# The depthwise convolution of a two-layer hybrid trunk on GpSimd: moved ahead of three weight subtractions, and its multiplications given a second operation

## The reference, cut to what matters

```python
z = _rms(h, norm1_g[l]) @ w_in[l]
ya = _attention_group(za, q_norm_g[l], k_norm_g[l], attn_sinks[l])
yr = _rwkv_group(zr, rwkv_mu[l], ...)
yc = _conv_group(zc, conv_w[l], conv_b[l], conv_ln_g[l], conv_ln_b[l])
h = h + jnp.concatenate([ya, yr, yc], axis=-1) @ w_out[l]
h = h + _peer(_rms(h, norm2_g[l]), peer_wq[l], peer_keys[l], peer_u[l], peer_v[l])

def _conv_group(z, conv_w, conv_b, ln_g, ln_b):
    u = z[..., :CONV_CH] * jax.nn.sigmoid(z[..., CONV_CH:])
    u = lax.conv_general_dilated(u, conv_w[:, None, :], window_strides=(1,), padding=[(CONV_K - 1, 0)],
                                 feature_group_count=CONV_CH) + conv_b
    return jax.nn.silu(_layernorm(u, ln_g, ln_b))
```

## Time and profile before

| What | Value |
|---|---|
| Median of 3 runs | 2122.08 us (2120.01, 2122.08, 2127.78) |
| Span of the profiled execution | 2125.6 us |
| PE busy, of the span | 1976.9 us, 93% |
| DVE busy | 1458.0 us, 69% |
| POOL busy | 1289.0 us, 61% |
| ACT busy | 963.9 us, 45% |
| Mixers of layer 0, from the end of the input projection to the output projection | about 96 to 233 us |
| Mixers of layer 1 | about 1155 to 1297 us |

### The profile page before, as it was taken

One profiled execution on the slowest core, in us unless ns is written; L12 is line 12 of the kernel. 1 busy time (PEld: TensorE's weight loads), 2 busy tenths in 40 slices (PEclk: granted clock), 3 DMA queues, 4 the chain that ended last, 5 costly groups with the idle time before them and its releaser, 6 DMA issues.

```text
span 2125.6 us, 43559 instructions
## 1 busy us (share of the span) xinstructions
PE 1976.9 (93%) x16496; PEld 1888.4 (89%) x16496; DVE 1458.0 (69%) x2763; ACT 963.9 (45%) x1645; POOL 1289.0 (61%) x667
## 2 busy tenths in 40 slices
PE   6857899999999999999998577999999999999999
PEld 6855899999999999999988466999999999999998
DVE  2773419994777788788757634199727777887886
ACT  5512446554333354555554124465543333555553
POOL 3798377998666633233047983789986666332430
PEclk9977899999999999999999679999999999999999
DMA  4400255565444598888743002555654445998995
GB/s 159 124 2 1 80 169 159 179 196 169 147 145 145 152 353 313 289 308 320 241 144 110 1 1 80 179 168 182 185 187 136 145 147 192 347 326 300 311 344 154
DMA packets 106236, 387.48 MB, mean 182 GB/s; under 512 B 11792, under 2 KB 12048, under 8 KB 105744
## 3 DMA queue, kind: packets, MB, share of 16 engines
q1 hardware_dynamic: 87696, 318.93, 45.8%
q0 software_dynamic: 18432, 67.12, 8.6%
HBM read 384.95 MB, written 1.05 MB: 182 GB/s over the span
## 4 chain that ended last, share of the span: by engine, by line
PE 60%; POOL 24%; issue 13%; DVE 1%; ACT 1%; DMA 1%; SPq 0%; POOLq 0%; ACTq 0%
PE ps L881 60%; POOL w_lo L544 14%; POOL arena L560 6%; POOL arena L569 4%; DMA arena<-lora_c 1%; POOL arena L556 0%; ACT w_hi L627 0%; DVE h L1791 0%; DVE x L1371 0%; SPq L509 0%; DVE sel L1677 0%; ACT L745 0%; ACT L602 0%; DVE x_lo L1364 0%; DVE h L1790 0%
## 5 line engine op out<-in xcount | busy, mean ns | idle before, releaser
L881 PE MATMUL ps<-x_hi,w_hi 128*128 128x240 f32 (+5 forms) x4768 | 1435.2, 325 | 29.4 <-POOL w_lo L544 10.7
L881 PE MATMUL ps<-x_hi,w_lo 128*128 128x240 f32 (+3 forms) x4768 | 1306.3, 274 | 0.0
L544 POOL TENSOR_TENSOR w_lo<-w,w_hi 128x1024 fp32r<-128x1024 f32 x346 | 868.1, 2526 | 414.7 <-ACT w_hi L627 414.4
L881 PEld LDWEIGHTS ps<-x_hi,w_hi 128*128 128x128 f32 x4768 | 905.2, 190 | 83.9 <-issue 15.2
L881 PEld LDWEIGHTS ps<-x_hi,w_lo 128*128 128x128 f32 x4768 | 909.8, 191 | 0.0
L627 ACT CAST w_hi<-w 128x1024 fp32r<-128x1024 f32 x596 | 623.2, 1046 | 348.3 <-PE ps L881 223.4
L881 PE MATMUL ps<-x_lo,w_hi 128*128 128x240 f32 (+3 forms) x2720 | 756.4, 278 | 0.0
L881 PEld LDWEIGHTS ps<-x_lo,w_hi 128*128 128x128 f32 x2720 | 519.8, 191 | 0.6
L1748 DVE TENSOR_TENSOR w_lo<-w,w_hi 128x1024 fp32r<-128x1024 f32 x250 | 305.5, 1222 | 114.8 <-ACT w_hi L627 114.4
L881 PE MATMUL ps<-arena 64*64 64x64 f32 (+9 forms) x2496 | 175.3, 276 | 59.7 <-ACT arena L769 21.1
L881 PEld LDWEIGHTS ps<-arena 64*64 64x64 f32 (+6 forms) x2496 | 151.5, 171 | 81.2 <-ACT arena L769 21.7
(11 more groups left out here) (185 smaller groups left out, 1699.1 us busy)
## 6 DMA issues: line engine op xcount, KB each, us to landing
w<-u_c SPq DMA_DIRECT2D x256, 512.0 KB, 3.6
w<-v_c SPq DMA_DIRECT2D x256, 512.0 KB, 4.4
w<-w_c SPq DMA_DIRECT2D x84, 512.0 KB, 3.6
arena<-keys_c SPq DMA_DIRECT2D x2, 1024.0 KB, 6.8
arena<-mix_c SPq DMA_DIRECT2D x2, 632.0 KB, 7.9
h<-h SPq DMA_DIRECT2D x1, 1088.0 KB, 5.1
out<-x SPq DMA_DIRECT2D x4, 256.0 KB, 2.2
arena<-lora_c SPq DMA_DIRECT2D x2, 256.0 KB, 8.0
```

What stands on the lines that cost most here:

```text
L544: g.tensor_tensor(low_of(l, n, wlo_t), low_of(l, n, wraw_t), high_of(l, n).bitcast(F32), ALU.subtract).then_inc(s_lo, 1)
L881: return nc.tensor.matmul(out_, lhsT, rhs, start=start, stop=stop, skip_group_check=True)
```

## The change

The three low halves 18, 19 and 20, which POOL made ahead of the convolution, are made behind it. And the multiplications of taps 1 to 30 get a second operation, the addition of the constant 0.0; tap 0 keeps its bias.

```diff
             for l in range(DEPTH):
-                lows(l, 0 if l == 0 else AHEAD, NZ + AHEAD)
+                lows(l, 0 if l == 0 else AHEAD, NZ)
 
                 pool.wait_ge(s_ea, l * (NZ + NQ) + ZQ)
...
                         ins = g.tensor_scalar(dst[:, j, :], cu[:, j, k:k + T], vcol(l, "conv_w", j * CONV_K + k),
-                                              vcol(l, "conv_b", j) if k == 0 else None, ALU.mult,
-                                              *((ALU.add,) if k == 0 else ()))
+                                              vcol(l, "conv_b", j) if k == 0 else 0.0, ALU.mult, ALU.add)
...
-                lows(l, NZ + AHEAD, NP)
+                lows(l, NZ, NP)
```

## The result

The changed kernel takes 2133.65 us (median of 9 runs), the kernel before 2125.99 us (9 runs). The ratio is 1.0038, with a 95% interval of 1.0026 to 1.005: slower by 8.1 us (5.5 to 10.6), where 2122 was forecast in a range up to 2129. It lies within the 0.5% that I had called no change, and outside the range. Part of the distance to 2122 was in the start of the sum: the three runs it was built on have a median of 2122.08 us, the nine of now 2125.99. The profiled execution after has a span of 2131.8 us against 2125.6; in the run after, the reported time is 1.85 us longer than the span.

A forecast was written before the change was run, and what follows sets the result against it. DVE's attention steps and ACT's exponentials were taken to bound the convolution's end. Ends -3.0, hold-ups in between +2.8 and PE's clock +0.9 gave +0.7 us on 2122.08: 2122 us, range 2112 to 2129.

The forecast's parts named there:

- The end of the convolution was not on the path: End of the convolution, layer 0: covered by DVE's attention until 208.95 and ACT's exponentials; ending 32 us earlier counted 0.
- 6.72 us of TensorE's wait: PE's wait for the convolution's last addition, layer 0: predicted to become waits for DVE, worth 0.
- The hold-ups in DVE's full stretch: DVE at about 110 to 135 us in layer 0: denser POOL additions cost +1.4 us a layer, +2.8 in all.
- ACT's cast within 2 us of 229.26: Sign at the mixers' end: ACT's cast of the mixed tokens stays there; 5 us or more earlier would refute the forecast.
- the 0.56 I took: Multiplication with a second operation on POOL: 0.56 us, like tap 0's, saving 24 us of POOL a layer.
- the 0.96 of the other bound: Multiplication no faster with the constant: 0.96 us, convolution ends at 200; rival forecast 2121 us, chance 0.12.
- the relief at the ends: DVE rows beside the last additions and PE's wait at the start: hold-ups vanish, -3.0 us over both layers.
- TensorE's transposes at 221.40 took 1.97, as forecast: Eight PE transposes after the convolution's sum, at 215.22 before: expected 1.97 us instead of 1.09, +0.9 us.
- the moved low halves: Three POOL low halves put behind the convolution, 2.4 to 2.9 us each: not needed before the output projection after 229.26.
- the hold-ups in between: Four hit places in DVE's full stretch, layer 0, about 4.5 us: 0.31 more of it, +1.4 us a layer.
- TensorE's clock, +0.9 us: PE's transposes late in the mixers run at the lower clock: +0.9 us; other bound, 2.4 GHz throughout, -4.6 together.
- That denser additions hit DVE and the clock more often: Rival: over twice the hold-ups in DVE's full stretch, as many in following steps, 6 us a layer: 2134 us, chance 0.04.

The follow-up runs named there:

- number 2: Kernel before with only the three low halves moved behind the convolution, multiplications left as they were: 2126.37 us, ratio 1.0005.
- The form alone: Kernel before with only the added 0.0 as second operation of the multiplications, low halves still ahead of the convolution: 2130.53 us, ratio 1.0017.
- 4: Changed kernel with each pair of multiplications of taps 1 to 30 done twice: 2130.64 us, ratio 1.0025 against the kernel before.
- 9: Kernel before with the second operation only, convolution started behind the first transposed inverses in both layers: 2128.47 us, ratio 1.0024.
- 10: Kernel before with the second operation, convolution started behind the first transposed inverses in layer 0, behind the normed keys in layer 1: 2125.44 us, ratio 1.0004.
- 5: Kernel before with the 60 additions replaced by instructions reading one input, partial sums left out: 2121.09 us, ratio 0.9981.
- 6: Changed kernel with the 60 additions replaced by instructions reading one input, partial sums left out: 2122.1 us, ratio 0.9981 against the kernel before.
- number 11: Kernel before with the second operation in layer 1 only, its convolution there started behind the normed keys: 2120.49 us, ratio 0.9976.
- 12: Layer 0 of the kernel before; layer 1 of the changed kernel with low halves held until the last RWKV state step: 2128.14 us, ratio 1.0013.
- number 3: Changed kernel with the three low halves held until the last RWKV state step is in PSUM: 2127.06 us, ratio 1.0008 against the kernel before.

## Why the prediction was wrong

**What held.** The end of the convolution was not on the path: 6.72 us of TensorE's wait were worth nothing, and the end came 35 us earlier for no gain. The hold-ups in DVE's full stretch, +1.4 us a layer, measured +1.1. Of what I had said would show the forecast, ACT's cast within 2 us of 229.26 is what failed: it came 7.05 us late. The second operation does make the multiplication faster: 0.48 us, a little under the 0.56 I took, and far from the 0.96 of the other bound. By the Trainium skill, GPSIMD Engine Reference (the statement stands in section 3.1, Elementwise — side-by-side cycle accounting), one and two operations would have cost alike; the rows after disagree with it as those before did. The start at 90.17 and the relief at the ends were right in kind: L1430 at 214.54 and L1436 at 219.01 are back at 0.17. TensorE's transposes at 221.40 took 1.97, as forecast.

**First step that failed: the moved low halves, "nobody asks for them before the output projection", priced at nothing.** I asked only who waits for them, and not what runs beside them. Having costed the additions by what they do to DVE's rows, I didn't cost the low halves by the same, though they too read two inputs, and are nearly twice as long. With the convolution over at 173.7 they run in 173.68 to 181.74, beside DVE's L1436 and L1438 (0.74 and 3.22 us instead of 0.17 and 1.36). Holding them back gave 6.4 us by the ratios. The same move without the form, where they stand at 199.60 to 207.05 in place of additions, costs nothing that can be measured (number 2).

**Second: the hold-ups in between were counted in too small a place.** I scaled four places in DVE's full stretch by the share of time that additions fill, and there the size was about right, +1.1 us a layer for +1.4. The steps behind that stretch stood at nothing. The form alone, which has the same ends to gain and no move, is slower by 3.7 us, where the terms of my sum without the start's give -2.2 + 2.8 + 0.9 = +1.5 and its full stretch shows 0.55 a layer. Numbers 4 and 9 have the full stretch 0.9 and 1.0 us a layer shorter than before and are 3.8 and 3.6 us slower all the same. One row that I had left out is L1430 at 169.98 (1.29 instead of 0.17), 8 columns in the chain of the attention. Numbers 9 and 10 show that the additions can be made to cost 3.0 us less in layer 1, and numbers 5 and 6, without the second input and at half the length, left 1.0 of the 8 us.

**Third: TensorE's clock, +0.9 us.** I followed one pair of rows at the end of the mixers. In the profiles the clock moved rows all through the mixers: the 68 products at 150.53 and the 116 behind them took 2.3 us more after, and 2.5 more in number 11 without the change; 216 products took 12.26 us at 191.07, where before 208 of them took 10.48 at 184.50 and 8 more 0.45. Over all runs with their mean granted clock, one intercept for each kernel, 0.001 of mean clock goes with 1.0 us (residual 1.2 us); the change's runs had 0.9576 and those of before 0.961 on average, so of the difference about 3.4 us go together with the clock and some 5 don't. Whether the clock is the cause of the 3.4 or itself follows from the held rows this doesn't separate. Number 5 has the mean clock of before, 0.961, and is 3.6 us faster: that gain isn't the clock's. Of the 7.7 us between 11 and 12, 3.7 go together with it (0.9634 and 0.9597).

**The rivals.** That denser additions hit DVE and the clock more often, priced at 2134 and given 4 in 100, is nearest to what happened. It lacked the low halves, which by number 3 are the larger part, and its doubled hold-ups in the full stretch didn't come: the loss is in the steps that follow. The Trainium skill, SBUF — State Buffer, section "Who interferes with whom", names a DVE instruction with two SBUF inputs as contending with any GpSimd instruction that reads SBUF. For the two-input ones on GpSimd the rows here agree (1.5 against 0.49). Beside one-input instructions rows of 0.57 to 0.89 stand where 0.49 is the size's own (number 6): there is some loss, but a small one. I had quoted the rule for additions and multiplications, and it covers the low halves too; beside them the row of 1.36 us took 3.22.

**What stays open.** Held back, the low halves gave 6.4 us, and the rows that I can name for them are 2.4 in layer 0. What the form alone loses behind DVE's full stretch, some 2.5 us of 3.7, has no row of its own either. The rest may be TensorE's clock behind the late step at 179.60; number 12 says that a profile of layer 1 can't be used for it. A held row ahead of a busy piece that then took long was seen three times (numbers 4, 9 and 10, 140 products in 11.92, 12.18 and 12.33 us), and in the change two held rows came ahead of the same 140 in 8.53; that the one brings the other about wasn't tried by itself.

## What to carry to other kernels

Work that is moved off the critical path still has to be priced by what it runs beside: ask of each two-input instruction on GpSimd which DVE rows share its time, and count each of them up to its full length. A faster helper that nobody waits for is worth nothing at its end, and can cost at its start; use the slack to try it behind the stretch where DVE is full, as number 11 does in layer 1, and layer by layer, since the same step lost in layer 0. When the effect sought is under 0.5%, take medians of ten runs (three gave 2122.08 us for the kernel before, nine 2125.99) and use the profile for the mechanism only. Look there for a piece that repeats: the same code gave 119.4 to 124.0 us over the whole mixers, and 32.31 to 32.34 where DVE alone sets the pace.

## What was unexpected of the hardware

A multiplication of 128 x 272 with a second operation took 0.48 us on GpSimd and without one 0.96; the constant addend is faster than the column of vectors (0.56 with the bias). A copy or update of 8 to 16 columns on DVE, 0.17 us by itself, took up to 1.3 us beside an addition on GpSimd. L1430 of the change ended at 171.27 and the addition beside it at 171.25, L1431 before at 208.54 and 208.52: what is lost is the rest of the other instruction and not a share of its own length. It goes the other way too: in number 6 a pair of multiplications beside DVE's two-input rows from L1378 on, at 113.70, took 1.94 us instead of 0.96.

```profile
114.34 1.94 POOL L560 TENSOR_SCALAR arena<-arena,vecs 128x272 f32<-128x272 f32 x2
...
117.30 0.96 POOL L560 TENSOR_SCALAR arena<-arena,vecs 128x272 f32<-128x272 f32 x2
```
